# Inverse transforms of a long convolution: the high and low part of one table side by side in one matmul of 272 columns

## The reference, cut to what matters

```python
def fftconv(v, kf, skip):
    L = v.shape[1]
    vf = jnp.fft.rfft(v.astype(jnp.float32), n=2 * L, axis=1)
    y = jnp.fft.irfft(vf * kf[None], n=2 * L, axis=1)[:, :L]
    return y + v.astype(jnp.float32) * skip.astype(jnp.float32)

def hyena_mixer(u, x1, x2, kf, skip):
    z = fftconv(u, kf[:, 0], skip[0])
    z = x1.astype(jnp.float32) * z
    z = fftconv(z, kf[:, 1], skip[1])
    return (x2.astype(jnp.float32) * z).astype(u.dtype)
```

## Time and profile before

| | |
|---|---|
| median of 3 runs | 1132.85 us (1132.75 to 1133.38) |
| the profiled execution | 1132.56 us |
| its span, first to last instruction | 1130.7 us |
| PE busy | 1105.2 us (98%), 7158 matmuls |
| DVE busy | 771.9 us (68%) |
| ACT busy | 567.6 us (50%) |

### The profile page before, as it was taken

How to read it: one execution, slowest core, us unless ns; L and a number is a source line. 1 busy time by engine, 2 the same in 40 slices (tenths; PEclk the granted TensorE clock), 3 DMA queues, 4 the chain that set the end, 5 groups by cost and what they waited for, 6 DMA issues and landing times.

```text
span 1130.7 us, 17228 instructions
## 1 busy us (share of the span) xinstructions
PE 1105.2 (98%) x7158; PEld 1006.0 (89%) x7158; DVE 771.9 (68%) x1151; ACT 567.6 (50%) x787; POOL 61.8 (5%) x98
## 2 busy tenths in 40 slices
PE   4999999999999999999999999999999999999997
PEld 2999999999999999999999988888888888888885
DVE  6778888778788688786788885555555455455654
ACT  6565555556545456465564554443444444344443
POOL 4030000300001300002000000000000000000000
PEclk9999999999999999999999999999999999999999
DMA  8654443644335534335543475555555555556652
GB/s 317 233 139 168 149 150 122 203 169 150 123 139 187 177 130 150 134 138 187 176 142 131 153 276 186 190 185 199 202 190 186 186 191 188 200 202 246 239 186 111
DMA packets 30493, 201.54 MB, mean 178 GB/s; under 512 B 3872, under 2 KB 4192, under 8 KB 7744
## 3 DMA queue, kind: packets, MB, share of 16 engines
q1 hardware_dynamic: 25024, 180.16, 45.3%
q0 software_dynamic: 5248, 19.77, 5.3%
q10 hardware_dynamic: 144, 0.52, 0.1%
HBM read 195.19 MB, written 5.24 MB: 177 GB/s over the span
## 4 chain that ended last, share of the span: by engine, by line
PE 74%; DVE 15%; ACT 6%; issue 4%; DMA 0%; ACTq 0%; DVEq 0%
PE ps L574 23%; PE ps L575 23%; PE ps L576 23%; DVE w_lo L1328 4%; ACT w_hi L988 2%; DVE prod L1569 1%; DVE prod L1570 1%; PE ps L598 1%; PE ps L579 1%; DVE k_lo L1328 1%; DVE prod L1571 1%; DVE y_lo L1328 1%; DVE prod L1572 1%; ACT y_hi L1189 1%; DVE hm L1415 1%
## 5 line engine op out<-in xcount | busy, mean ns | idle before, releaser
L1328 DVE TENSOR_TENSOR w_lo<-raw,w_hi 128x1024 fp32r<-128x1024 f32 x336 | 409.0, 1230 | 258.4 <-ACT w_hi L988 258.1
L988 ACT ACTIVATE w_hi<-raw 128x1024 fp32r<-128x1024 f32 x336 | 351.2, 1056 | 344.0 <-PE ps L576 342.3
L574 PE MATMUL ps<-xn_hi,w_hi 128*128 128x272 f32 (+2 forms) x1280 | 367.3, 287 | 0.0
L575 PE MATMUL ps<-xn_lo,w_hi 128*128 128x272 f32 (+2 forms) x1280 | 365.4, 285 | 0.0
L576 PE MATMUL ps<-xn_hi,w_lo 128*128 128x272 f32 (+2 forms) x1280 | 365.1, 285 | 0.0
L574 PEld LDWEIGHTS ps<-xn_hi,w_hi 128*128 128x128 f32 x1280 | 242.0, 189 | 2.0
L575 PEld LDWEIGHTS ps<-xn_lo,w_hi 128*128 128x128 f32 x1280 | 241.8, 189 | 0.7
L576 PEld LDWEIGHTS ps<-xn_hi,w_lo 128*128 128x128 f32 x1280 | 242.0, 189 | 0.0
L574 PE MATMUL ps<-w_hi,xg_hi 128*128 128x512 f32 x352 | 137.2, 390 | 0.0
L576 PE MATMUL ps<-w_hi,xg_lo 128*128 128x512 f32 x352 | 137.0, 389 | 0.0
L575 PE MATMUL ps<-w_lo,xg_hi 128*128 128x512 f32 x352 | 136.9, 389 | 0.0
(11 more groups left out here) (265 smaller groups left out, 1394.0 us busy)
## 6 DMA issues: line engine op xcount, KB each, us to landing
raw<-w_stream SPq DMA_DIRECT2D x168, 1024.0 KB, 4.9
branch_y<-ystage POOLq DMA_DIRECT2D x12, 256.0 KB, 3.4
y_raw<-branch_y POOLq DMA_DIRECT2D x3, 1024.0 KB, 6.5
xin<-x SPq DMA_DIRECT2D x2, 1024.0 KB, 6.5
w4s<-w POOLq DMA_DIRECT2D x16, 128.0 KB, 5.9
absd<-decay POOLq DMA_DIRECT2D x8, 256.0 KB, 6.0
h<-x POOLq DMA_DIRECT2D x2, 1024.0 KB, 8.4
rows_t<-rpb POOLq DMA_DIRECT2D x8, 219.0 KB, 6.2
```

Of the source, the lines that this page charges most:

```text
L574: mm(out_ap, a_hi, b_hi, start=first, stop=False)
L575: mm(out_ap, a_hi, b_lo, start=False, stop=False)
L988: A(w_hi[:, w % 2, part, :], raw[:, w % 4, 1024 * part:1024 * part + 1024], ACT.Copy).then_inc(hi_done, 1)
L1328: return V.tensor_tensor(dst, src, hi.bitcast(F32), ALU.subtract)
```

## The change

For the even half, the table's high and low part stand side by side in `sym_hi` (272 columns), so that high·high and high·low are one matmul, into columns 0 to 135 and 136 to 271 of the PSUM bank. The third product (the spectrum's low part by the table's high part) and the remainder stay matmuls of 136 columns. The even half then has two partial sums; DVE copies the one to SBUF and adds the other before the unfolding as it was. The odd half keeps its three matmuls, its sums lie in columns 272 to 407. `sym_hi` grows from 7 to 8 times 272 columns, `sym_lo` shrinks from 4 to 3 times, so the loaded bytes stay the same.

```diff
+    hi, lo = two_parts(...)
+    wide = [part[:, at:at + HL] for b in (2 * L, 3 * L) for part, at in ((hi, b), (lo, b), (hi, b + HL))]
+    sym = (np.concatenate([hi[:, 0:2 * L]] + wide + [hi[:, 4 * L:]], axis=1),
+           np.concatenate([lo[:, 0:2 * L], lo[:, 2 * L + HL:3 * L], lo[:, 3 * L + HL:4 * L]], axis=1))
...
             def inverse():
                 for i in range(2):
-                    for ri in range(2):
-                        out_ap = ps[:, 4 + i, HL * ri:HL * ri + HL]
-                        for f in range(2):
-                            back = 2 * L + HL * (2 * f + ri)
-                            three(out_ap, y_hi[:, f, ri, 128 * i:128 * i + 128], y_lo[:, f, ri, 128 * i:128 * i + 128],
-                                  sym_hi[:, back:back + HL], sym_lo[:, back:back + HL], f == 0, False)
-                        back = 6 * L + HL * ri
-                        last = stacked(out_ap, y_hi[0:STACK, 2, ri, 128 * i:128 * i + 128], sym_hi[0:STACK, back:back + HL],
-                                       False, True)
+                    chans = slice(128 * i, 128 * i + 128)
+                    even, odd = ps[:, 4 + i, 0:HL], ps[:, 4 + i, L:L + HL]
+                    for f in range(2):
+                        back = 2 * L + 3 * HL * f
+                        mm(ps[:, 4 + i, 0:L], y_hi[:, f, 0, chans], sym_hi[:, back:back + L], start=f == 0, stop=False)
+                        mm(even, y_lo[:, f, 0, chans], sym_hi[:, back:back + HL], start=False, stop=False)
+                    stacked(even, y_hi[0:STACK, 2, 0, chans], sym_hi[0:STACK, 7 * L:7 * L + HL], False, True)
+                    for f in range(2):
+                        back, low = 3 * L + 3 * HL * f, 2 * L + HL * f
+                        three(odd, y_hi[:, f, 1, chans], y_lo[:, f, 1, chans], sym_hi[:, back:back + HL],
+                              sym_lo[:, low:low + HL], f == 0, False)
+                    last = stacked(odd, y_hi[0:STACK, 2, 1, chans], sym_hi[0:STACK, 7 * L + HL:8 * L], False, True)
                 last.then_inc(inv_mm, 1)
...
             def unfold(c, src, skip, p0):
 
+                even = prod[:, 0, :, 0:HL]
+                link(V.tensor_copy(even, ps[:, 4:6, HL:L]))
+                link(V.tensor_tensor(even, even, ps[:, 4:6, 0:HL], ALU.add))
                 for i in range(2):
                     by = params[:, c * 2 + skip + i:c * 2 + skip + i + 1]
-                    V.scalar_tensor_tensor(u[:, i, p0:HL], src[:, i, p0:HL], by, ps[:, 4 + i, p0:HL], ALU.mult, ALU.add)
-                    ins = V.scalar_tensor_tensor(u[:, i, HL:L][:, ::-1], src[:, i, HL:L][:, ::-1], by, ps[:, 4 + i, 0:HL],
+                    V.scalar_tensor_tensor(u[:, i, p0:HL], src[:, i, p0:HL], by, even[:, i, p0:HL], ALU.mult, ALU.add)
+                    ins = V.scalar_tensor_tensor(u[:, i, HL:L][:, ::-1], src[:, i, HL:L][:, ::-1], by, even[:, i, :],
                                                  ALU.mult, ALU.add)
                 link(ins)
-                V.tensor_tensor(u[:, :, p0:HL], u[:, :, p0:HL], ps[:, 4:6, HL + p0:L], ALU.add)
-                V.tensor_tensor(u[:, :, HL:L][:, :, ::-1], u[:, :, HL:L][:, :, ::-1], ps[:, 4:6, HL:L],
+                V.tensor_tensor(u[:, :, p0:HL], u[:, :, p0:HL], ps[:, 4:6, L + p0:L + HL], ALU.add)
+                V.tensor_tensor(u[:, :, HL:L][:, :, ::-1], u[:, :, HL:L][:, :, ::-1], ps[:, 4:6, L:L + HL],
                                 ALU.subtract).then_inc(unfolded, 1)
```

More of the change, by code:

```diff
@@ L145, in constants @@
     back = [np.concatenate([even.T[p:p + n], odd.T[p:p + n]], axis=1) for p, n in TOK]
-    sym = two_parts(np.concatenate([even[:128], odd[:128], back[0], back[1]], axis=1),
-                    np.concatenate([np.concatenate([even[128:], none]), np.concatenate([none, odd[128:]]), back[2]], axis=1))
+    hi, lo = two_parts(np.concatenate([even[:128], odd[:128], back[0], back[1]], axis=1),
+                       np.concatenate([np.concatenate([even[128:], none]), np.concatenate([none, odd[128:]]), back[2]], axis=1))
+    wide = [part[:, at:at + HL] for b in (2 * L, 3 * L) for part, at in ((hi, b), (lo, b), (hi, b + HL))]
+    sym = (np.concatenate([hi[:, 0:2 * L]] + wide + [hi[:, 4 * L:]], axis=1),
+           np.concatenate([lo[:, 0:2 * L], lo[:, 2 * L + HL:3 * L], lo[:, 3 * L + HL:4 * L]], axis=1))
     lag = FPOS.astype(np.float64)[:, None] * om[None, :]
@@ L223, in build @@
     mix_at = at[0]
-    sym_hi = place("sym_hi", [128, 7 * L], F32R)
-    sym_lo = place("sym_lo", [128, 4 * L], F32R)
+    sym_hi = place("sym_hi", [128, 8 * L], F32R)
+    sym_lo = place("sym_lo", [128, 3 * L], F32R)
     fch_hi = place("fch_hi", [128, 2, 2 * FK], F32R)
@@ L494, in _ @@
                        ftok_lo[:, :, :].rearrange("p a n -> p (a n)"), 6 * NG)
-            load_table("sym", sym_in, sym_hi[:, :], sym_lo[:, :], 7 * L)
+            load_table("sym", sym_in, sym_hi[:, :], sym_lo[:, :], 8 * L)
             pool.wait_ge(mask_landed, 16)
@@ L694, in forward @@
                     out_ap = ps[0:fn, bank, CC * ri:CC * ri + CC]
-                    main, rest = L * ri + fp, (4 + ri) * L + fp
+                    main, rest = L * ri + fp, (5 + ri) * L + fp
                     three(out_ap, sym_hi[:, main:main + fn], sym_lo[:, main:main + fn], uT_hi[:, ri, :], uT_lo[:, ri, :],
```

## The result

The changed kernel took 1139.03 us (median of 5 runs, 1136.82 to 1139.46) beside 1132.75 for the kernel before: a ratio of 1.0048, with an interval of 1.0034 to 1.0062. The forecast was 1133.7, and no change. The profiled execution is the fastest of the five, 1136.82 us, which is 4.3 above that of the kernel before.

A forecast was written before the change was run, and what follows sets the result against it. PE was taken to bound the kernel after first inverses, DVE and ACT before second unfoldings. -1.56 + 2.82 - 0.39 = +0.87 us on the profiled 1132.56, median 0.29 above: 1133.7 us, range 1132.0 to 1135.6.

The forecast's parts named there:

- What bounds the kernel: PE sets the pace after each chunk's first inverse; DVE and ACT from there to the second unfolding, chunks 0 to 2.
- what PE saves: Each inverse, 4 wide and 20 narrow matmuls instead of 28 narrow: 2.72 us for 3.11, 0.39 less.
- The rule of the Trainium skill that was weighed there: Isolated matmul costs its columns at 2.4 GHz plus 2.5 ns: some 0.01 us saved, sum +2.8 us; rejected on the trace.
- What DVE pays: Each unfolding gets a linked copy and sum of 128x272: 0.94 us, bounds 0.78 to 1.10.
- The Trainium skill's rule that SBUF sources cost less: Fixed 58 cycles for SBUF, 120 for PSUM: four skip-term instructions 0.26 us cheaper, sum nearer +0.1; no change was taken.
- The sum: First inverses 4 x -0.39, second inverses of chunks 0 to 2 3 x +0.94, chunk 3's second -0.39: +0.87 us.
- the pricing of the stop: PE's standstill before the second unfolding, chunks 0 to 2, grows from 0.84 to 2.17 us, adding 3 x 0.94 = +2.82.
- The signs that it named: Inverse about 2.7 us, DVE groups of 0.43 and 0.44, unfolding waits near 6 in total, chunk distance up 0.55.
- The unfolding does not end with the inverse: Denies rival: second unfolding begins earlier or its extra 0.94 is hidden, all 8 x 0.39 count, 1129.7 us; chance 0.05.
- PE does gain: Denies rival: a wide matmul costs two narrow ones, 3 x 0.94 remain, 1135.7 us; chance 0.04.
- the first unfolding stays hidden: Denies rival: DVE's delay reaches PE at the scores after slab 11, up to 3.8 on top, 1137.5 us; chance 0.07.
- the stop isn't given back later: Denies rival: PE's later waits for attention's scaling, chunks 1 to 3, each shrink by 0.55, 1132.0 us; chance 0.04.

The follow-up runs named there:

- e5_filled_stop: Changed kernel with twelve spare 136-column matmuls in front of PE's wait for the second unfolding, chunks 0 to 2: 1133.77 us beside 1132.4, ratio 1.0012.
- f0: Changed kernel with wide matmul, copy and sum only in each chunk's first inverse and chunk 3's second: 1131.32 us beside 1132.71, ratio 0.9987.
- e1: Changed kernel without VectorE's copy and sum, the table's low part left out of the even half: 1131.25 us beside 1132.4, ratio 0.9985.
- e3: Changed kernel with two 512-column matmuls moved in front of PE's wait for the second unfolding: 1134.98 us beside 1132.71, ratio 1.0022.
- e2: Kernel before plus the copy and sum in front of every unfolding, result unused, no wide matmul: 1136.56 us beside 1132.4, ratio 1.0037.
- f3: Kernel before, second unfolding of chunks 0 to 2 moved earlier on DVE, two 512-column matmuls before PE's wait: 1129.55 us beside 1132.57, ratio 0.9975.
- a3: One more profiled execution of the changed kernel, unaltered: 1138.73 us.

## Why the prediction was wrong

*What bounds the kernel, and what PE saves: right.* PE leads after the first inverse, DVE and ACT before the second unfolding. An inverse is 0.39 shorter. The rule of the Trainium skill that was weighed there ("TensorE: Matmul & The Clock Gate", section "Back-to-back issue gap"), on the spacing of isolated matmuls, would have had no gain; the traces of before and after don't agree with it (3.08 and 2.69 us). The section itself says that this formula comes out too low for small matmuls in a stream of weight loads and matmuls, which is the case here.

*What DVE pays: right.* 0.94 for the copy and the sum. With them the way from the start of `fi_lo` to PE's next matmul is 3.66 us (186.66 to 190.32) where it was 2.68 (186.96 to 189.64), 0.98 more, so 0.04 lie beside the two. A chunk came out 0.60 longer (153.23 less 152.63) where the sum had 0.55. The Trainium skill's rule that SBUF sources cost less ("VectorE: DVE Perf Modes", section "The TRN2 errata") is not borne out for these instructions: 128x136 with the skip term takes 347 to 351 ns with a source in PSUM (before) and 355 to 358 with all in SBUF (changed), each a mean of eight.

*The sum: right as far as it goes.* The runs of the changed kernel without a fall take 1133.5 to 1133.8; the forecast was 1133.7. e5_filled_stop, in which PE's idle time is filled and nothing else changed, takes 1133.77. Against the kernel before as it was measured beside them these are some 1.0 and 1.4 more, where the sum had 0.87, so the agreement is one of about half a microsecond.

*The step that failed* is the pricing of the stop: "PE stands still for 0.84 + 0.39 + 0.94 = 2.17 instead of 0.84, and goes on 0.94 later than the chain: 3 x +0.94 = +2.82." The length was right (2.13), but it was priced as if PE went on at the speed at which it had stopped. In the kernel before, stops of 0.84 bring no fall. Stops of 1.7 to 2.3 bring one behind some of them, of 3.4 us at half the clock and 1.5 to 1.6 us lost, once of twice that. None in a run gives 1133.7, two give 1136.8, more give 1138.7 and up. The first five runs had none of the first kind, and so the median lies 5.3 above the forecast. No rival had this mechanism: the prediction does not name the clock at all, so what it does behind a longer stop was put at nothing without a reason. The signs that it named came out as it had them or nearly so (the inverse in 2.69 us, the two groups on DVE, the waits, the distance of the chunks without a fall); the clock was not among them.

*The rivals.* None held. The unfolding does not end with the inverse, PE does gain, the first unfolding stays hidden (f0), and the stop isn't given back later: the other wait of PE is unchanged, and grew slightly where PE came earlier (e1).

*What stays open:* behind which stop the clock falls, and why stops of 1.7 us in e3 brought falls in all eight runs when those of 1.8 us in e2 did not. The kernel is the same from one execution to the next, but the way from the clock's first rise to the first stop differs by up to 1.2 us in the four profiles of the changed kernel. In the seven profiles of stops from 1.7 to 2.3 us the fall behind the first stop goes with how long after that rise the stop ends (e3 above); that this decides was not tried.

## What to carry to other kernels

Price a stop of TensorE twice: by its length, and by what the clock may do behind it. Where the stops before are short and a change makes them longer, "no fall in the trace of before" is no evidence, and the page's row in tenths doesn't show a short fall; look at stretches of 2 us behind each stop. And when a change takes work from the leading engine and gives it to a second one, look at each place where the first already waits for the second: there the gain is lost and the cost counts in full, so make the change only at the other places, or first move the waiting work (here an order on DVE that filled its own wait for ACT, together with two matmuls of PE moved in front of its wait, was worth more than the change itself: 3.0 us in f3, against 1.4 for the change at its best places in f0; what each of the two is worth alone was not measured on the kernel before).

## What the runs showed of the hardware that was not expected

- A stop of about 2 us of TensorE can halve its granted clock (1.00 to 0.50) for 3.4 us, and not during the stop but 0.1 to 2.0 us after the work has resumed (stop until 190.32, fall at 192.3; in a3 stop until 343.80, fall at 343.9). That costs 1.5 to 1.6 us. After one stop (a3_changed_one_look) the low clock lasted twice as long and cost 3.1.
- The fall behind the first stop came 163.8 us after the clock's first rise in three profiles of three kernels, though the stops before it ended 0.3 us apart by that measure.
- Twelve spare matmuls inside such a stop, with 0.85 us of standstill left, kept the clock at 0.998 or 0.999 in ten of eleven runs (0.997 in the other).
- The same program on the same chip has runs without a fall and runs with several, so its times lie in groups 2 to 3 us apart. The median of few runs depends on which groups they fall into (1139.03 of five, 1136.4 of twelve).
